# The SSD mixer of an eight-block model: new order of its scalar, vector and matmul work, and the head's own cumulative sum subtracted by matmuls

## The chip, the cores and the metric

The kernel runs on one core of one Trainium2 chip. A core has a matmul engine (PE), a vector engine (DVE), a scalar engine (ACT), a general engine (POOL) and a queue engine that here only issues DMAs (SP). Each runs its own list of instructions in the order in which the program wrote them, and the engines meet only at semaphores. The metric is the device time of one execution in microseconds; smaller is better.

## The reference

The model applies several blocks to an activation of 512 positions by 1024 channels: an SSD mixer with its FFN, an RG-LRU mixer with its FFN, and later blocks of other kinds. Only the SSD mixer is touched. In the names of the kernel it is:

```python
proj = u @ w_in                              # 1024 -> z (2048), xbc (3072), dt (32)
xbc  = silu(causal_dwconv(xbc, conv_w, conv_b))      # 4 taps
xs, bm, cm = split(xbc)                      # 2048 channels, and B and C: 4 groups x 128 each
dt = softplus(dt_raw + dt_bias);  a = -exp(a_log)
cs = cumsum(dt * a) within each chunk of 128 positions    # per head, 32 heads of 64 channels
scores  = (C_l . B_s) * exp(cs_l - cs_s)     # for s <= l in the chunk, else 0
y_diag  = scores @ (xs * dt)
states  = B^T @ (xs * dt * exp(cs_last - cs))
y_off   = exp(cs) * (C @ entering_state)     # states carried over the 4 chunks
y = y_diag + y_off + d_skip * xs
g = y * silu(z);  g = g * rsqrt(mean(g * g) over each group of 512 channels) * norm_w
out = g @ w_out
```

## The kernel before

Activations lie with channels on the 128 partitions and the 512 positions along the free axis. A matmul in float32 is replaced by three in float32r: weight and activation are each split into a high part and a rest, and high x high, high x rest and rest x high are summed. A weight unit is 128 x 1024 (eight blocks of 128 x 128). SP loads it into one of five ring slots when the unit five places earlier is used up, ACT rounds it to the high part (`split_hi`, line 319), POOL subtracts to get the rest (`lows`, line 2335), and PE runs 24 matmuls of 512 columns on it (`pe_tile`, lines 374 to 376).

The mixer has two stretches on PE.

**The convolution stretch.** PE makes 24 tiles of xbc, in turn in PSUM banks 0 to 3. For each tile DVE scales (line 1168, into `ctap`), ACT multiplies by the last tap (line 1024), DVE adds three taps (line 1173) and ACT applies SiLU (line 1015), which frees the bank. The dt work (`dt_chain`: softplus, the cumulative sum `csT`, and its split into three float32r parts in `cs3`) stands as one block on ACT and DVE, ahead of tile 8. After each of the tiles 15 to 22 PE transposes two finished x tiles (`x_natural`, line 839, into banks 4 and 5), and waits before each for the DVE product of the tile two places earlier (line 1152, semaphore `xdt_ok`). DVE does these products behind the convolution of the same turn:

```python
            if 16 <= t:
                x_natural(2 * t - 32)
                x_natural(2 * t - 31)
```

**The pair loop.** Sixteen turns, each for one pair of heads `i` (one tile of 128 channels); four turns make a group. In turn `i` PE does: `y_entering(i)` (line 921), four blocks of z tile `i+1` (`z_blocks`, lines 855 to 857, in PSUM banks 0 and 1 in turn), `y_diagonal(i)` (line 932), `decay_rows(i+1)` (lines 899, 900 and 913) and the other four blocks. `decay_rows` selects the head's row of `cs3` and spreads it over all partitions, adds the causal mask by a second matmul, and for the pair makes the rows for `ec` in bank 6. ACT exponentiates each chunk with the column `nat` (minus the head's own cumulative sum) as its bias: four instructions of 128 columns a head (line 1048). DVE multiplies by C.B (`t1`, line 1235), scales and sums y (1226, 1228, 1210) and gates it with z (`gate`, 1198 to 1203). In turn `i` DVE does the gate of pair `i-1`, behind the products of pair `i`, and that gate frees the bank of z tile `i-1`. Once a group there are `b_natural` (876), `c_b` (867), three `states` (889, between which DVE's `entering` and POOL's `decayed` stand), `squares` (941, 943), `inverse` on ACT and `normed` on DVE. POOL builds `selp` (`pair_rows`), sums squares and makes the rest parts of g (`low_g`).

After the loop `ssd_out` begins (from line 396), and the rest of the program follows.

Of the kernel before, what the change touches and what calls it, by code (L numbers as in the profile page):

```python
# [146 lines left out]
def build_program(nc, dram, out_dram):  # L147
    ctx = ExitStack()
    with ctx:
# [4 lines left out]
        for name, size in (("cols", NCOL * 4 + (-NCOL * 4) % 32), ("ident", 512), ("ones", 512), ("mask_r", 512),  # L154
                           ("neg_diag", 512), ("pair_mask", 512), ("eps", 32), ("x", 16 * KB), ("h", 32 * KB),
                           ("m", 16 * KB), ("raw", 4 * RING * KB), ("whi", 4 * RING * KB), ("nacc", 2 * KB),
                           ("ipre", 2 * KB), ("ident_r", 512), ("sel3", 128), ("sqg", 2 * KB),
# [14 lines left out]
        sel3 = at("sel3", place["sel3"], [P, 32], F32R)  # L172
# [640 lines left out]
        def ssd_pe(pe):  # L813
# [77 lines left out]
            def decay_rows(i):  # L891
# [5 lines left out]
                for e in range(2):  # L897
# [3 lines left out]
                              mask_r[:].unsqueeze(1).broadcast_to((P, NC, P)), start=False, stop=True).then_inc(p_cs, 1)  # L901
# [50 lines left out]
            c_b(0)  # L952
            b_natural(0, 0)
# [35 lines left out]
        def ssd_act(act, own):  # L989
# [3 lines left out]
            def dt_chain():  # L993

                act.wait_ge(dt_dve, 1)
                act.activation(dd[:, 0, :], dd[:, 0, :], ACT.Identity, bias=col("dt_bias")).then_inc(dt_act, 1)
                act.wait_ge(dt_act, 1)
                own.link(act.activation(dd[:, 1, :], dd[:, 0, :], ACT.Abs))
                act.activation(dd[:, 1, :], dd[:, 1, :], ACT.Exp, scale=-1.0).then_inc(dt_act, 1)
                act.activation(acol[:, 0:1], col("a_log"), ACT.Exp).then_inc(dt_act, 1)  # L1000
                act.wait_ge(dt_dve, 2)
                act.activation(dd[:, 3, :], dd[:, 2, :], ACT.Ln).then_inc(dt_act, 1)
                act.wait_ge(dt_dve, 3)
                act.activation(dd[:, 1, :], dd[:, 1, :], ACT.Exp).then_inc(dt_act, 1)

                act.activation(cs3[:], csT[:], ACT.Copy).then_inc(dt_act, 1)
                act.wait_ge(dt_dve, 5)
                act.activation(cs_mid[:], dd[:, 0, :], ACT.Copy).then_inc(dt_act, 1)
                act.activation(cs3[32:64, :], dd[32:64, 0, :], ACT.Copy)
                act.wait_ge(dt_dve, 6)  # L1010
                act.activation(cs3[64:96, :], dd[64:96, 2, :], ACT.Copy).then_inc(dt_act, 1)

            def silu(t):
                act.wait_ge(s_c1, 3 * t + 3)
# [1640 lines left out]
```

## Time and profile before

| | us |
|---|---|
| median of 3 runs | 3316.71 |
| lowest and highest run | 3313.44, 3317.73 |
| the profiled execution's own time | 3312.69 |
| its span, first to last instruction | 3310.8 |
| PE busy in the span | 3030.8 |
| DVE, ACT, POOL busy | 1374.4, 1206.5, 1352.6 |
| convolution stretch, first tiles to its last matmul | until 240.9 |
| pair loop | 257.57 to 518.98 |

A busy share is an average over stages with different limits. PE instructions overlap, so the time of a run of matmuls is read from start to start; the duration of one is longer than its share. The granted clock (PEclk, 1.00 is 2.4 GHz, 0.50 is 1.2 GHz) is a mean over the stretch shown.

### The profile page before, as it was taken

What the parts mean: (1) busy time and instruction counts of PE and PEld (TensorE: products, weight loads), DVE (VectorE), ACT (ScalarE), POOL (GpSimd) and SP (SyncE); (2) the same over time, 40 slices, a digit from 0 to 9 for tenths busy, and PEclk for the clock granted to TensorE, in tenths of its full rate; (3) what the DMA queues carried; (4) which work ended last, traced back from release to release, by engine and by line L of the source; (5) the groups of instructions that cost most, each with busy time, mean ns of one, the idle gap of its engine ahead of it and who ended that gap; (6) DMA issues with size and microseconds to landing.
All of it is one profiled execution on the core that took longest, in us unless ns stands there. A gap on an engine that the chain in (4) does not pass through costs nothing.

```text
span 3310.8 us, 33604 instructions
## 1 busy us (share of the span) xinstructions
PE 3030.8 (92%) x13380; PEld 2459.0 (74%) x13380; DVE 1374.4 (42%) x2011; ACT 1206.5 (36%) x1751; POOL 1352.6 (41%) x724
## 2 busy tenths in 40 slices
PE   8667778999999988899999999798999989999998
PEld 6555557788888766688888877697888866778886
DVE  5533332354154077355145246673422345433132
ACT  5312343543244256354234243103323334343232
POOL 5222225444444436554444444303444443054443
PEclk9878889999999989999999999669999999999999
DMA  3111002222222212222222222001223222022322
GB/s 129 57 38 32 32 26 70 83 96 96 96 96 97 95 58 74 76 96 96 96 96 96 96 83 96 1 1 64 96 88 104 84 85 67 9 92 92 102 91 81
DMA packets 74171, 253.10 MB, mean 76 GB/s; under 512 B 8352, under 2 KB 8352, under 8 KB 74016
## 3 DMA queue, kind: packets, MB, share of 16 engines
q1 hardware_dynamic: 73008, 247.55, 22.8%
q10 hardware_dynamic: 1008, 3.41, 0.3%
q8 instruction: 107, 1.75, 0.2%
q14 instruction: 48, 0.39, 0.0%
HBM read 248.83 MB, written 2.10 MB: 76 GB/s over the span
## 4 chain that ended last, share of the span: by engine, by line
PE 84%; DVE 8%; ACT 3%; issue 2%; DMA 2%; POOL 1%; POOLq 0%; DVEq 0%; ACTq 0%; SPq 0%
PE bank L374 21%; PE bank L375 21%; PE bank L376 21%; PE bank L1639 3%; PE bank L396 2%; PE bank L398 2%; PE bank L397 2%; PE bank L855 1%; PE bank L856 1%; PE bank L857 1%; PE bank L932 1%; POOL wlo L2335 1%; DVE lth L1484 1%; DVE bank L1173 1%; DVE t L1235 1%
## 5 line engine op out<-in xcount | busy, mean ns | idle before, releaser
L2335 POOL TENSOR_TENSOR wlo<-raw,whi 128x1024 fp32r<-128x1024 f32 (+2 forms) x497 | 1133.0, 2282 | 1817.9 <-ACT whi L319 1817.9
L319 ACT ACTIVATE whi<-raw 128x1024 fp32r<-128x1024 f32 (+2 forms) x497 | 500.0, 1007 | 1155.1 <-DMA raw<-in_f_up 490.2
L374 PE MATMUL bank<-h_hi,whi 128*128 128x512 f32 x2240 | 886.9, 396 | 20.8 <-ACT xbc L1015 13.4
L375 PE MATMUL bank<-h_lo,whi 128*128 128x512 f32 x2240 | 879.5, 393 | 0.0
L376 PE MATMUL bank<-h_hi,wlo 128*128 128x512 f32 x2240 | 877.9, 392 | 0.0
L374 PEld LDWEIGHTS bank<-h_hi,whi 128*128 128x128 f32 x2240 | 426.2, 190 | 114.1 <-ACT xbc L1015 14.3
L375 PEld LDWEIGHTS bank<-h_lo,whi 128*128 128x128 f32 x2240 | 426.0, 190 | 90.6 <-issue 2.4
L376 PEld LDWEIGHTS bank<-h_hi,wlo 128*128 128x128 f32 x2240 | 425.5, 190 | 89.9
L374 PE MATMUL bank<-act_hi,whi 128*128 128x512 f32 x864 | 341.3, 395 | 0.8 <-POOL wlo L2335 0.8
L376 PE MATMUL bank<-act_hi,wlo 128*128 128x512 f32 x864 | 341.2, 395 | 0.0
L375 PE MATMUL bank<-act_lo,whi 128*128 128x512 f32 x864 | 341.1, 395 | 0.0
L722 DVE TENSOR_TENSOR tg<-bank,ipre 128x512 f32<-128x512 f32 x108 | 74.6, 691 | 298.3 <-PE bank L376 251.1
L374 PEld LDWEIGHTS bank<-act_hi,whi 128*128 128x128 f32 x864 | 162.3, 188 | 40.3 <-POOL wlo L2335 1.3
L376 PEld LDWEIGHTS bank<-act_hi,wlo 128*128 128x128 f32 x864 | 162.4, 188 | 39.0
L375 PEld LDWEIGHTS bank<-act_lo,whi 128*128 128x128 f32 x864 | 162.4, 188 | 38.8
L855 PE MATMUL bank<-h_hi,whi 128*128 128x512 f32 x128 | 66.5, 520 | 71.3 <-DVE xbc L1203 71.3
L678 ACT ACTIVATE bank<-tg,cols 128x512 f32<-128x512 f32 x108 | 84.6, 783 | 115.9 <-DVE tg L722 115.9
L396 PE MATMUL bank<-h_hi,whi 128*128 128x512 f32 x192 | 82.8, 431 | 42.5 <-DVE h_lo L584 40.8
L742 DVE TENSOR_TENSOR xT<-bank,xT 128x512 f32<-128x512 f32 x32 | 22.1, 692 | 198.8 <-PE bank L376 198.8
L727 DVE TENSOR_TENSOR tv<-bank,ipre 128x512 f32<-128x512 f32 x64 | 44.2, 691 | 133.4 <-PE bank L376 133.4
L855 PEld LDWEIGHTS bank<-h_hi,whi 128*128 128x128 f32 x128 | 30.8, 241 | 85.7 <-DVE xbc L1203 77.9
L708 DVE SCALAR_TENSOR_TENSOR bank<-tg,cols,bank 128x511 f32<-128x511 f32 x108 | 81.5, 755 | 30.6 <-ACT bank L678 29.8
(448 smaller groups left out, 3907.6 us busy)
## 6 DMA issues: line engine op xcount, KB each, us to landing
raw<-in_f_up SPq DMA_DIRECT2D x216, 512.0 KB, 3.5
raw<-in_f_dn SPq DMA_DIRECT2D x64, 512.0 KB, 3.5
raw<-in_ssd_xbc SPq DMA_DIRECT2D x24, 512.0 KB, 3.5
raw<-in_f_dn SPq DMA_DIRECT2D x32, 384.0 KB, 3.0
raw<-in_lru_in SPq DMA_DIRECT2D x20, 512.0 KB, 3.5
raw<-in_ev_in SPq DMA_DIRECT2D x20, 512.0 KB, 3.5
raw<-in_f_dn SPq DMA_DIRECT2D x32, 320.0 KB, 2.9
raw<-in_ssd_z SPq DMA_DIRECT2D x16, 512.0 KB, 3.5
```

What stands on the lines that cost most here:

```text
L319: act.activation(whi[:, s, 0:WIDTH[u]], raw[:, s, 0:WIDTH[u]], ACT.Copy).then_inc(hi_done, 1)
L374: pe.matmul(out, wh, hi, start=kt == 0, stop=False)
L375: pe.matmul(out, wh, lo, start=False, stop=False)
L376: last = pe.matmul(out, wl, hi, start=False, stop=kt == n - 1)
L396: pe.matmul(out, wh, hi, start=kt == 0, stop=False)
L397: pe.matmul(out, wh, lo, start=False, stop=False)
L678: act.activation(bg[:], tg[:, e, :], ACT.Identity, bias=self.prm_col(j + prev, 3), scale=self.prm_col(j + prev, 2)).then_inc(self.tap, 1)
L708: dve.scalar_tensor_tensor(out=dst[:, 1:T], in0=src[:, 0:T - 1], scalar=self.prm_col(j + prev, 4 * v + 1), in1=dst[:, 1:T], op0=ALU.mult, ...
L722: dve.tensor_tensor(tg[:, e, :], bg[:], ipre[:], ALU.mult).then_inc(self.u, 1)
L855: pe.matmul(o, wh, hi, start=kt == 0, stop=False)
L1639: last = pe.matmul(o, wb[rows, n, c, j, :], steps(ev[rows, j, :], m, 1 - n), start=n == 1, stop=n == 0)
L2335: pool.tensor_tensor(wlo[:, s, 0:n], raw[:, s, 0:n], whi[:, s, 0:n].bitcast(F32), ALU.subtract)\
```

## The change

`sel3` gets a second half, columns 32 to 63, with the selection matrix times -1. `decay_rows` adds four float32r matmuls a head, one a chunk: the stationary operand is the chunk of `cs3`, the moving operand the negated selection column spread over 128 columns. They subtract the head's own cumulative sum of each partition. The exponential has no bias any more and is one instruction of 512 columns a head.

The order changes as follows. The dt work is cut into steps ahead of tiles 3, 5, 12, 14, 16 (ACT) and 4, 6 to 11, 13, 15 (DVE). DVE's `x_natural` products stand ahead of the convolution of their turn. B's transposes and C.B of group 0 move between xbc tiles. In the pair loop DVE begins with the two products by C.B, does the whole gate of pair `i` in turn `i` (scale, silu, sum of y, product), and `normed` and `entering` are moved around it. On ACT the exponentials of the heads come ahead of `ec`, and tanh and square are those of pair `i`. On PE `squares` comes a turn earlier; POOL's order follows.

```diff
--- before.py
+++ after.py
...
@@ -898,12 +898,16 @@
                     h = 2 * i + e
                     pe.matmul(bank[4 + e][:], sel3[0:96, h:h + 1].broadcast_to((96, P)), cs3[0:96, :], start=True, stop=False)
                     pe.matmul(bank[4 + e][:].rearrange("p (c l) -> p c l", c=NC), ident_r[:],
-                              mask_r[:].unsqueeze(1).broadcast_to((P, NC, P)), start=False, stop=True).then_inc(p_cs, 1)
+                              mask_r[:].unsqueeze(1).broadcast_to((P, NC, P)), start=False, stop=False)
+                    for c in range(NC):
+                        last = pe.matmul(chunk(bank[4 + e], c), chunk(cs3[0:96, :], c),
+                                         sel3[0:96, 32 + h:33 + h].broadcast_to((96, P)), start=False, stop=c == NC - 1)
+                    last.then_inc(p_cs, 1)
                 g, q = (i - 1) // 4, (i - 1) % 4
                 w(pe, p_ec, i)
                 if i == 0:
                     pe.wait_ge(g_ent, 2)
-                elif q == 1:
+                elif q == 0:
                     w(pe, gn_inv, g)
                 elif q == 2 and g + 1 < SSD_G:
                     pe.wait_ge(g_bn, g + 2)
@@ -949,8 +953,10 @@
                 if 15 <= t <= 22:
                     x_natural(2 * t - 30)
                     x_natural(2 * t - 29)
-            c_b(0)
-            b_natural(0, 0)
+                if t == 20:
+                    b_natural(0, 0)
+                if t == 22:
+                    c_b(0)
             z_blocks(2)
             states(0, 0)
             states(0, 1)
@@ -961,7 +967,7 @@
             for i in range(NX):
                 g, q = i // 4, i % 4
                 y_entering(i)
-                if q == 1 and g:
+                if q == 0 and g:
                     squares(g - 1, i + 1)
                 if q == 2 and g + 1 < SSD_G:
                     b_natural(g + 1, i + 1)
@@ -990,63 +996,65 @@
             stage["ssd_dt"].split_ahead(0)
             st, zt = stage["ssd_xbc"], stage["ssd_z"]
 
...
+            def dt_step(t):
+
+
+                if t == 3:
+                    act.wait_ge(dt_dve, 1)
+                    act.activation(dd[:, 0, :], dd[:, 0, :], ACT.Identity, bias=col("dt_bias")).then_inc(dt_act, 1)
+                    act.wait_ge(dt_act, 1)
+                    own.link(act.activation(dd[:, 1, :], dd[:, 0, :], ACT.Abs))
+                    act.activation(dd[:, 1, :], dd[:, 1, :], ACT.Exp, scale=-1.0).then_inc(dt_act, 1)
+                    act.activation(acol[:, 0:1], col("a_log"), ACT.Exp).then_inc(dt_act, 1)
+                elif t == 5:
+                    act.wait_ge(dt_dve, 2)
+                    act.activation(dd[:, 3, :], dd[:, 2, :], ACT.Ln).then_inc(dt_act, 1)
+                elif t == 12:
+                    act.wait_ge(dt_dve, 3)
+                    act.activation(dd[:, 1, :], dd[:, 1, :], ACT.Exp).then_inc(dt_act, 1)
+                    act.activation(cs3[:], csT[:], ACT.Copy).then_inc(dt_act, 1)
+                elif t == 14:
+                    act.wait_ge(dt_dve, 5)
+                    act.activation(cs_mid[:], dd[:, 0, :], ACT.Copy).then_inc(dt_act, 1)
+                    act.activation(cs3[32:64, :], dd[32:64, 0, :], ACT.Copy)
+                elif t == 16:
+                    act.wait_ge(dt_dve, 6)
+                    act.activation(cs3[64:96, :], dd[64:96, 2, :], ACT.Copy).then_inc(dt_act, 1)
+                    act.wait_ge(tr_dt, 2)
+                    act.activation(etot[:].rearrange("p a b -> p (a b)"), bank[5][:, 0:P], ACT.Exp).then_inc(dt_act, 1)
+
+            def keep_b(g):
+                act.wait_ge(g_bt, g + 1)
+                act.activation(bn[:].rearrange("p c l -> p (c l)"), bank[6][:], ACT.Copy).then_inc(g_bn, 1)
+
+            def keep_cb(g):
+                act.wait_ge(g_cb, g + 1)
+                act.activation(xbc[:, 16 + g, :], bank[7][:], ACT.Copy).then_inc(g_cbm, 1)
 
             def silu(t):
                 act.wait_ge(s_c1, 3 * t + 3)
                 act.activation(xbc[:, t, :], st.bank(t)[:], ACT.Silu).then_inc(st.free(t), 1)
 
             for t in range(24):
-                if t == 8:
-                    dt_chain()
-                if t == 16:
-                    act.wait_ge(tr_dt, 2)
-                    act.activation(etot[:].rearrange("p a b -> p (a b)"), bank[5][:, 0:P], ACT.Exp).then_inc(dt_act, 1)
+                dt_step(t)
                 act.wait_ge(s_u, t + 1)
                 act.activation(st.bank(t)[:], ctap[:, t % 2, :], ACT.Identity, bias=col("ssd_conv", t * 5 + 4),
                                scale=col("ssd_conv", t * 5 + 3)).then_inc(s_tap, 1)
                 st.split_ahead(t)
                 if t:
                     silu(t - 1)
+                if t == 22:
+                    keep_b(0)
             silu(23)
 
...
             def exps(i):
+                for e in range(2):
+                    h = 2 * i + e
+                    act.wait_ge(p_cs, h + 1)
+                    act.activation(bank[4 + e][:], bank[4 + e][:], ACT.Exp).then_inc(p_E, 1)
                 act.wait_ge(p_c2, i + 1)
                 w(act, p_om, i)
                 act.activation(ec[:], bank[6][:], ACT.Exp).then_inc(p_ec, 1)
-                for e in range(2):
-                    h = 2 * i + e
-                    act.wait_ge(p_cs, h + 1)
-                    for c in range(NC):
-                        b = chunk(bank[4 + e], c)
-                        last = act.activation(b, b, ACT.Exp, bias=nat[:, 0, c, h:h + 1])
-                    last.then_inc(p_E, 1)
 
             def z_tanh_of(i):
                 act.wait_ge(z_scaled, i + 1)
@@ -1074,15 +1082,13 @@
                 act.wait_ge(gn_n, j + 1)
                 act.activation(g_hi[:, j, :], xbc[:, j, :], ACT.Copy).then_inc(gn_hi, 1)
 
-            keep_b(0)
             keep_cb(0)
             exps(0)
             for i in range(NX):
                 g, q = i // 4, i % 4
-                if i:
-                    z_tanh_of(i - 1)
-                if q == 1 and g:
+                if q == 0 and g:
                     inverse(g - 1)
+                z_tanh_of(i)
                 if q == 2 and g + 1 < SSD_G:
                     keep_b(g + 1)
                 if q >= 2 and g:
@@ -1092,10 +1098,7 @@
                     exps(i + 1)
                 if q == 2 and g + 1 < SSD_G:
                     keep_cb(g + 1)
-                if i:
-                    square(i - 1)
-            z_tanh_of(NX - 1)
-            square(NX - 1)
+                square(i)
             inverse(SSD_G - 1)
             for k in range(4):
                 high(12 + k)
@@ -1111,38 +1114,49 @@
             st.freed(dve, 0)
             dve.engine_nop().then_inc(dt_dve, 1)
 
...
+            def dt_step(t):
+
...
             st, zt = stage["ssd_xbc"], stage["ssd_z"]
 
@@ -1156,14 +1170,16 @@
 
             for t in range(24):
                 b = st.bank(t)
-                if t == 8:
-                    dt_chain()
+                dt_step(t)
                 if t == 15:
 
                     dve.wait_ge(tr_dt, 1)
                     own.link(dve.tensor_scalar(nat[:, 0].rearrange("p b c -> p (b c)"), bank[4][:, 0:P], -1.0, None, ALU.mult))
                     dve.tensor_copy(nat[:, 1:3].rearrange("p a b c -> p (a b c)"), bank[4][:, P:3 * P]).then_inc(dt_dve, 1)
                     dve.wait_ge(dt_dve, 7)
+                if t >= 16:
+                    x_natural(2 * t - 32)
+                    x_natural(2 * t - 31)
                 st.tile_ready(dve, t)
                 dve.tensor_tensor(ctap[:, t % 2, :], b[:], ipre[:], ALU.mult).then_inc(s_u, 1)
                 dve.wait_ge(s_tap, t + 1)
@@ -1173,13 +1189,10 @@
                     dve.scalar_tensor_tensor(
                         out=b[:, n + 1:T], in0=ctap[:, t % 2, 0:T - n - 1], scalar=col("ssd_conv", t * 5 + 2 - n),
                         in1=b[:, n + 1:T], op0=ALU.mult, op1=ALU.add).then_inc(s_c1, 1)
-                if 16 <= t:
-                    x_natural(2 * t - 32)
-                    x_natural(2 * t - 31)
-
-            def entering(g):
-
-                for z in range(3):
+
+            def entering(g, first, end):
+
+                for z in range(first, end):
                     dve.wait_ge(g_ds, 3 * g + z + 1)
                     if z == 0:
                         dve.tensor_copy(ent[:, 0, :], bank[7][:]).then_inc(g_ent, 1)
...
@@ -1217,31 +1234,35 @@
 
             st.freed(dve, 22)
             dve.memset(bank[2][:, 0:P], 0.0).then_inc(p_xd, 1)
-            entering(0)
+            entering(0, 0, 3)
             y = bank[2][:, P:T]
             for i in range(NX):
                 g, q = i // 4, i % 4
+                dve.wait_ge(g_cbm, g + 1)
+                w(dve, p_y, i)
+                for e in range(2):
+                    dve.wait_ge(p_E, 2 * i + e + 1)
+                    dve.tensor_tensor(t1[:, e, :], bank[4 + e][:], xbc[:, 16 + g, :], ALU.mult).then_inc(p_S, 1)
                 dve.wait_ge(p_off, i + 1)
                 dve.wait_ge(p_ec, i + 1)
                 dve.tensor_tensor(y, y, ec[:, P:T], ALU.mult).then_inc(p_om, 1)
                 dve.wait_ge(p_om, i + 1)
                 dve.scalar_tensor_tensor(out=xbc[:, i, :], in0=xbc[:, i, :], scalar=col("ssd_d", i), in1=bank[2][:],
                                          op0=ALU.mult, op1=ALU.add).then_inc(p_xd, 1)
-                if i:
-                    y_sum(i - 1)
-                dve.wait_ge(g_cbm, g + 1)
-                for e in range(2):
-                    dve.wait_ge(p_E, 2 * i + e + 1)
-                    dve.tensor_tensor(t1[:, e, :], bank[4 + e][:], xbc[:, 16 + g, :], ALU.mult).then_inc(p_S, 1)
-                if i:
-                    gate(i - 1)
-                if q in (1, 2) and g:
-                    normed(4 * g + 2 * q - 6)
-                    normed(4 * g + 2 * q - 5)
+                z_scale(i)
+                if q == 1 and g:
+                    normed(4 * g - 2)
+                    normed(4 * g - 1)
                 if q == 3 and g + 1 < SSD_G:
-                    entering(g + 1)
-            y_sum(NX - 1)
-            gate(NX - 1)
+                    entering(g + 1, 0, 2)
+                z_silu(i)
+                y_sum(i)
+                gated(i)
+                if q == 0 and g:
+                    normed(4 * g - 4)
+                    normed(4 * g - 3)
+                if q == 3 and g + 1 < SSD_G:
+                    entering(g + 1, 2, 3)
             for k in range(4):
                 normed(12 + k)
             so = stage["ssd_out"]
@@ -2398,30 +2419,28 @@
                 if j in (1, 3):
                     u = lows(u, u + 1)
             zt = stage["ssd_z"]
-            u = lows(u, stage["ssd_xbc"].u0 + 23 + RING)
+            u = lows(u, stage["ssd_xbc"].u0 + 20 + RING)
             decayed(0, 0)
             decayed(0, 1)
-            u = lows(u, u + 1)
-            decayed(0, 2)
+            u = lows(u, stage["ssd_xbc"].u0 + 24 + RING)
             pair_rows(0)
             pair_rows(1)
+            decayed(0, 2)
             for i in range(NX):
                 g, q = i // 4, i % 4
-                if i:
-                    u = lows(u, zt.u0 + i + RING)
-                    if i + 1 < NX:
-                        pair_rows(i + 1)
+                if i + 2 < NX:
+                    pair_rows(i + 2)
+                if i and (i - 1) % 4 in (1, 2):
+                    square_sum(i - 1)
+                u = lows(u, zt.u0 + i + 1 + RING)
+                if q == 2 and g + 1 < SSD_G:
+                    decayed(g + 1, 0)
+                    decayed(g + 1, 1)
                 if q >= 2 and g:
                     low_g(4 * g + 2 * q - 8)
                     low_g(4 * g + 2 * q - 7)
-                if q == 2 and g + 1 < SSD_G:
-                    decayed(g + 1, 0)
-                    decayed(g + 1, 1)
                 if q == 3 and g + 1 < SSD_G:
                     decayed(g + 1, 2)
-                if (i - 1) % 4 in (1, 2) and i:
-                    square_sum(i - 1)
-            u = lows(u, zt.u0 + NX + RING)
             for k in range(4):
                 low_g(12 + k)
             u = squares(u, stage["ssd_out"], post0.stat, ffn_pre0.stat)
@@ -2483,7 +2502,8 @@
             act.wait_ge(c_rest, 16)
             act.activation(mask_r[:], pre_mask[:], ACT.Copy)
             act.activation(ident_r[:], ident[:], ACT.Copy)
-            act.activation(sel3[:], pre_sel[:], ACT.Copy)
+            act.activation(sel3[:, 0:32], pre_sel[:], ACT.Copy)
+            act.activation(sel3[:, 32:64], pre_sel[:], ACT.Copy, scale=-1.0)
             norm0.stat.root(act, ipre[:])
             ssd_act(act, own)
             ffn_pre0.act(act, stage["ssd_out"])
```

## Rows read from the trace of the kernel before

**Rows 1.** The page: the chain that ended last, by engine.

```profile
PE 84%; DVE 8%; ACT 3%; issue 2%; DMA 2%; POOL 1%; POOLq 0%; DVEq 0%; ACTq 0%; SPq 0%
```

**Rows 2.** Busy time by stretch: start:end, length, PE, PEld, DVE, ACT, POOL, clock, DMA.

```profile
45.00:86.60 41.60, 40.69 (x180) 33.33 (x178) 25.63 (x33) 23.75 (x30) 17.12 (x8) 1.00 0.28 90
86.60:99.50 12.90, 0.37 (x3) 0.01 (x1) 9.96 (x19) 6.81 (x10) 1.90 (x1) 0.66 0.11 41
130.60:137.46 6.86, 0.04 (x2) 0.04 (x1) 2.95 (x4) 3.88 (x5) 3.78 (x2) 0.83 0.24 76
137.46:240.90 103.44, 70.89 (x256) 57.53 (x257) 29.00 (x42) 17.66 (x22) 18.71 (x10) 0.75 0.11 36
257.57:518.98 261.41, 187.40 (x855) 143.49 (x853) 99.49 (x150) 89.44 (x207) 68.01 (x54) 0.85 0.10 33
```

**Rows 3.** PE's waits (total us, times, longest) in 40:137, 137:257 and 257:519.

```profile
PE bank L374 <- ACT xbc L1015: 13.4, 2, 12.5
...
PE bank L839 <- DVE xdt L1152: 32.5, 7, 4.7
PE bank L839 <- ACT etot L1022: 6.8, 1, 6.8
PE bank L889 <- ACT xbc L1037: 4.1, 1, 4.1
...
PE bank L855 <- DVE xbc L1203: 71.3, 14, 5.9
```

**Rows 4.** Timeline of PE, one transposing turn: start, us, what, count, idle before.

```profile
137.46 1.94 PE L839 MATMUL bank<-ident,xbc 128*128 128x128 f32 x8 [6.82 <-ACT etot L1022]
...
140.05 0.63 PE L376 MATMUL bank<-h_hi,wlo 128*128 128x512 f32 x1
140.47 0.63 PE L374 MATMUL bank<-h_hi,whi 128*128 128x512 f32 x1
...
145.48 0.39 PE L375 MATMUL bank<-h_lo,whi 128*128 128x512 f32 x1
145.71 0.39 PE L376 MATMUL bank<-h_hi,wlo 128*128 128x512 f32 x1
150.75 1.94 PE L839 MATMUL bank<-ident,xbc 128*128 128x128 f32 x8 [4.65 <-DVE xdt L1152]
```

**Rows 5.** Timeline of PE, one turn of the pair loop.

```profile
402.72 1.58 PE L932 MATMUL bank<-t,xdt 128*64 128x128 f32 x16
...
408.24 0.83 PE L921 MATMUL bank<-xbc,ent 128*128 128x128 f32 x6
408.90 1.02 PE L941 MATMUL bank<-nacc,ones 128*128 128x512 f32 x2
409.76 1.02 PE L943 MATMUL bank<-sqg,ones 128*128 128x512 f32 x2
414.98 0.79 PE L855 MATMUL bank<-h_hi,whi 128*128 128x512 f32 x1 [4.20 <-DVE xbc L1203]
```

**Rows 6.** Timeline of PE, between the two stretches.

```profile
241.13 1.06 PE L867 MATMUL bank<-xbc 128*128 128x128 f32 x8
242.02 0.60 PE L876 MATMUL bank<-ident,xbc 128*128 128x128 f32 x4
242.38 0.48 PE L855 MATMUL bank<-h_hi,whi 128*128 128x512 f32 x1
```

**Rows 7.** Groups of instructions in 0:620: busy us, mean ns, idle before.

```profile
L1048 ACT ACTIVATE bank<-bank,nat 128x128 f32<-128x128 f32 x128 | 34.2, 364 | 0.0
...
L2362 POOL TENSOR_TENSOR xdd<-xdt,nat 128x512 f32<-128x512 f32 x12 | 12.3, 1039 | 1.8 <-PE bank L889 1.8
...
L1210 DVE TENSOR_TENSOR xbc<-bank,xbc 128x512 f32<-128x512 f32 x16 | 10.9, 684 | 0.0
...
L1042 ACT ACTIVATE ec<-bank 128x512 f32<-128x512 f32 x16 | 9.6, 598 | 112.9 <-PE bank L913 112.9
```

**Rows 8.** Busy time of a stretch of the last attention block, columns as in rows 2.

```profile
2799.00:2879.00 80.00, 77.06 (x409) 56.28 (x407) 47.73 (x161) 33.78 (x101) 0.74 (x1) 1.00 0.00 1
```

More of the change, by code:

```diff
@@ L171, in build_program @@
         ident_r = at("ident_r", place["ident_r"], [P, P], F32R)
[L172 removed]
+        sel3 = at("sel3", place["sel3"], [P, 64], F32R)
         sqg = at("sqg", place["sqg"], [P, T])
@@ L991, in ssd_act @@
             st, zt = stage["ssd_xbc"], stage["ssd_z"]
[L993 to L1011, printed above, removed]
@@ new lines, in dt_step @@
+            def dt_step(t):
+                if t == 4:
+                    dve.wait_ge(dt_act, 2)
+                    dve.tensor_scalar(v, u, 1.0, None, ALU.add).then_inc(dt_dve, 1)
+                elif t == 6:
+                    dve.wait_ge(dt_act, 4)
+                    own.link(dve.tensor_scalar(v, v, -1.0, 1e-30, ALU.add, ALU.max))
+                    own(dve.reciprocal(v, v))
+                elif t == 7:
+                    own.sync()
+                    own.link(dve.tensor_tensor(ln, ln, u, ALU.mult))
+                    own(dve.tensor_tensor(ln, ln, v, ALU.mult))
+                elif t == 8:
+                    own.sync()
+                    own.link(dve.tensor_scalar(v, u, -0.5, 1.0, ALU.mult, ALU.add))
+                    own(dve.tensor_tensor(v, v, u, ALU.mult))
+                elif t == 9:
+                    own.sync()
+                    own.link(dve.tensor_tensor(ln, ln, v, ALU.max))
+                    own(dve.scalar_tensor_tensor(out=dtT[:], in0=x, scalar=0.0, in1=ln, op0=ALU.max, op1=ALU.add))
+                elif t == 10:
+                    dve.wait_ge(dt_act, 3)
+                    own.link(dve.tensor_scalar(acol[:, 1:2], acol[:, 0:1], -1.0, None, ALU.mult))
+                    own.link(dve.tensor_scalar(x, dtT[:], acol[:, 1:2], None, ALU.mult))
+                    for c in range(NC):
+                        own(dve.tensor_tensor_scan(out=chunk(csT[:], c), data0=ones[:], data1=chunk(x, c), initial=0.0,
+                                                   op0=ALU.mult, op1=ALU.add))
+                elif t == 11:
+                    own.sync()
+                    cs3d = csT[:].rearrange("p (c l) -> p c l", c=NC)
+                    tot = cs3d[:, :, P - 1:P]
+                    dve.tensor_tensor(dd[:, 1, :].rearrange("p (c l) -> p c l", c=NC), tot.broadcast_to((P, NC, P)), cs3d,
+                                      ALU.subtract).then_inc(dt_dve, 1)
+                    dve.tensor_tensor(diag[:], ident[0:32, 0:32].unsqueeze(2).broadcast_to((32, 32, NC)),
+                                      tot[0:32].rearrange("p c l -> p l c").broadcast_to((32, 32, NC)),
+                                      ALU.mult).then_inc(dt_dve, 1)
+                elif t == 13:
+                    dve.wait_ge(dt_act, 6)
+                    dve.tensor_tensor(x, csT[:], cs3[:].bitcast(F32), ALU.subtract).then_inc(dt_dve, 1)
+                elif t == 15:
+                    dve.wait_ge(dt_act, 7)
+                    dve.tensor_tensor(v, x, cs_mid[:].bitcast(F32), ALU.subtract).then_inc(dt_dve, 1)
```

45 lines of the change are left out of this document (6 added, 39 removed).

## The prediction

> **What bounds the kernel now.** I read the page's chain first: PE ends most of it [rows 1]. Then the busy time by stretch, for where PE is not dense: in 45 to 86.6 us it is busy throughout at clock 1.00, but from 86.6 to 99.5 it stands, from 137.46 to 240.9 it is busy 71 of 103 us at clock 0.75, and in the pair loop 187 of 261 us at 0.85, with no other engine over 100 us [rows 2]. So neither stretch is bounded by an engine's work; both are bounded by waits. PE's waits give their names: 13.4 us for xbc's SiLU (the dt block on ACT and DVE), 6.8 us for `etot`, 32.5 us in 7 waits for the product `xdt`, 71.3 us in 14 waits for the gate of line 1203 [rows 3]. Last the timelines of PE. A wait costs more than its idle time: after one, the matmuls start 0.43 us apart (1.2 GHz), and only later 0.23 us apart (2.4 GHz) [rows 4]. Behind the mixer PE is dense, so what the mixer saves moves the end.
>
> **The dt steps.** The block's 12.9 us stall [rows 2] and the slow start behind it (about 8 matmuls 0.2 us too long, 1.6 us) go. The cover: before the block DVE was busy 25.6 us of 41.6 and ACT 23.8 us [rows 2]. A tile lasts 24 x 0.227 = 5.45 us, so DVE has about 2.1 us to spare in each. The block's DVE work, some 15 us (10.0 of it in the stall's row [rows 2]), is spread over 12 tiles with 25 us to spare, and a tile's bank is needed again only four tiles later. ACT switches its function table more often, inside the same slack. If that cover failed, up to 14.5 us would stay. The steps end with `etot` behind the tap and the weight split of tile 15, as before, and one more full-width copy stands ahead of it (0.6 us, as `ec` of [rows 7]): the wait of 6.9 us becomes 7.5. Sum: -12.9 - 1.6 + 0.6 = **-13.9 us** (ends: 0 and -20.8, the latter if the second wait went too).
>
> **The products `xdt` ahead of the convolution.** PE asks, before the transposes behind tile t, for products that DVE now does before it starts tile t's convolution, while PE makes that tile. The 4.65 us wait [rows 4] goes, and the clock stays up. One turn was 150.75 - 137.46 = 13.3 us [rows 4]. Eight transposes take about 8 x 0.11 = 0.9 (four take 0.36 in [rows 6]); with the tile, 6.35 us. DVE's turn is two products and five passes with a wait for ACT, about 5.3 us by 0.68 a pass [rows 7], so DVE does not become late. The first turn still starts slow: 13.3 - 4.65 = 8.65. With C.B and the transposes of B, now inside this stretch (0.89 and 0.36 [rows 6]): 8.65 + 7 x 6.35 + 1.25 = 54.3 against 103.4 [rows 2], **-49.1 us**. At 8.65 for all eight it would be -33. Between the stretches PE still waits for tile 23's SiLU and C.B's copy; it merely arrives earlier. I take 16.7 + 0.4 us there, **+0.4**.
>
> **The added matmuls.** Eight a pair, 128 in all, 96 x 128 by 128 columns in float32r. No row shows that shape. Below: the stream of 128 columns at the 512-column pitch of [rows 4] would be 0.227 / 4 = 0.06 us. Above: the whole 0.227. I take 0.111, the pitch of the 128-column instructions of line 867 (eight in 0.89 us [rows 6]), the nearest in shape: 0.89 us a pair, 14.2 us in all (7 to 29). The Trainium skill, "TensorE: Matmul & The Clock Gate", section "Back-to-back issue gap", gives about 81 ns for a 128-column matmul in a stream of load and matmul pairs; by that it would be 10.4 us. Its figure is not for float32r, and the row stands.
>
> **The pair loop.** Before, z tile i+1 waited for the gate of pair i-1, which DVE did in the same turn behind y_entering, the sum and the products. Now that gate ends in turn i-1. I walk a turn from the end of `y_diagonal(i-1)`, T. DVE: sum and gate, T+1.8; products of pair i need the exponentials. PE: selection, mask and new matmuls, the first head at about T+1.0, the second T+1.9, `ec`'s row T+2.1. ACT: each exponential 0.6 us at full width [rows 7] in place of four of 128 columns, so T+1.8 and T+2.7. DVE's products end at T+3.6. PE meanwhile has four z blocks, y_entering and four more, and wants the products at T+8.3. The gate that z tile i+1 needs was done at T+1.8, and is wanted at T+5.4. Queued behind DVE's new wait on the exponentials are y's scaling, the skip and the z scale; they would be late only if the exponentials came over 2 us later. So PE should be its own bound. Its turn without waits, at full clock: y_diagonal, decay_rows and four blocks 408.24 - 402.72 = 5.52, y_entering 0.66 [rows 5], four blocks 2.72, new matmuls 0.89: 9.8 us. DVE's work is 99.5 / 16 = 6.2 us a turn, ACT's 5.6, POOL's 4.3 [rows 2], all below.
>
> Fifteen turns 147; the last, without z blocks, 2.1; three times a group's own work (squares 1.72 and three states at 0.86 [rows 5], C.B and B 1.25 [rows 6], 5.55) 16.7. What is late next is POOL: `decayed(g+1, 2)` (1.04 us [rows 7]) stands behind the weight rest and two `low_g`, and PE wants its state right behind decay_rows; I allow 2 us in two groups, 4. Sum 170 against 261.4, **-91.6 us**. Here the shorter exponentials and `ec` being last cost nothing, hidden by PE's z blocks; without that cover the turn would be longer by their 1.8 us. The loads of SP follow the end of each tile and land before ACT's tanh, as before. The tail into `ssd_out` is bounded by PE's own first twelve blocks, so it is unchanged; the added table copy at the start lies in ACT's wait for PE.
>
> **Sum.** -13.9 - 49.1 + 0.4 - 91.6 = -154.2. Against the profiled execution (3312.7) that is 3158.5; the median of the runs is 4.0 above it (3316.7), so the forecast is **3163 us**.
>
> **Rivals.** (a) *Narrow matmuls cost as much as wide ones*, 0.227 us each: +14.9, **3178**. For: float32r is a mode of its own, and no narrow one is in the trace. Against: other 128-column instructions take half.
> (b) *A wait stays in the loop.* A turn has many crossings between four queues, and a late tanh (behind the weight split's DMA on ACT) or the products hold the gate. If half of the 5.1 us wait stays in 15 turns, 38 us, with some slow restart, 10: **3211**. For: DVE and ACT are strict queues and the walk leaves out latencies. Against: 3 us and more of room at each crossing.
> (c) *The clock stays at 1.2 GHz among transposes.* Seven turns would have 24 matmuls 0.2 us longer and transposes 0.9 longer, 5.7 x 7 = 40: **3203**. In this stretch the clock was 0.75 [rows 2], but the rows put the slow matmuls behind the waits; in the last attention, where transposes stand among matmuls without long waits, it is 1.00 [rows 8]. The same page of the Trainium skill, "Part 4: PE-mode transpose", says that transposing does not count as busy for the clock; by that rule this case would hold, and the last row speaks against it.
> (d) *The dt steps stall the tiles*: the ACT queue with its table switches falls behind by more than the four banks, and the 14.5 us stay: **3178**.
> (e) *Slower than before*: each new matmul holds PE, in that its stationary operand can't be brought in beside the open sum of the bank. It decides from 154 / 128 = 1.2 us each; at 1.3 us instead of 0.111 the time is 3163 + 152 = 3315, at 1.4 **3328**. The longest PE instruction in these rows takes 1.02 for two, so nothing speaks for it. That the change leaves the waits as they are (no order that PE sees altered) can be excluded only by the code: it would give about 3317 + 14 = 3331, with (e)'s side.
>
> **Chances.** Forecast 0.60 (its own range 3148 to 3175), (a) 0.14, (b) 0.13, (c) 0.05, (d) 0.05, (e) and no effect 0.03. The low end takes 0.06 us a matmul (-7), no POOL wait (-4) and the `etot` wait gone (-7): 3145, and I go to 3140; the high end takes in (a), (c), (d) and (b): 3213. Two runs of this kernel can be told apart from about 0.2%, 6.6 us: faster 0.97, within 0.2% 0.01, slower 0.02.
>
> **What would show it.** In the new profile: no wait over 2 us of line 374 before tile 16; one wait of some 7.5 us before the first transposes, none for `xdt`; turns of 6.4 us; clock 1.00 from there; turns of the pair loop of 9.8 us with no wait of the z blocks; the narrow matmuls 0.11 us apart; a wait of states for `xdd` in two or three groups. The forecast is wrong if the loop still shows z waits for the gate, or PE waits for the products by C.B, or the clock falls in it.

## The result and the profile after

The changed kernel takes **3148.2 us** (median; 3143.5 to 3150.8) against 3315.8 beside it: ratio **0.949** [0.948, 0.951]. The forecast of 3163 lies 14.8 us above it. The profiled execution took 3148.6 us, with a span of 3146.7 (before 3310.8). The page of the kernel after, the chain by engine, answers to [rows 1]:

```profile
PE 86%; DVE 7%; ACT 3%; DMA 1%; issue 1%; POOL 1%; POOLq 0%; DVEq 0%; ACTq 0%; SPq 0%
```

The busy time by stretch, columns as in [rows 2]. The first stretch is that of before's stall; then come the wait for `etot`, the turns with transposes, and the pair loop:

```profile
86.60:99.50 12.90, 12.09 (x53) 9.48 (x52) 10.95 (x17) 4.49 (x6) 5.00 (x3) 1.00 0.29 87
121.20:128.07 6.87, 0.00 (x1) 0.03 (x1) 2.49 (x4) 4.51 (x6) 3.34 (x2) 0.78 0.26 76
128.07:181.96 53.89, 53.89 (x268) 45.63 (x269) 30.39 (x44) 18.18 (x23) 18.71 (x9) 0.96 0.21 69
199.60:374.31 174.71, 171.45 (x975) 137.65 (x973) 98.63 (x151) 76.78 (x118) 70.56 (x55) 0.98 0.15 47
```

103.4 us became 53.9 and 261.4 became 174.7, with PE busy nearly throughout. PE's waits of the whole span, those in the mixer, answer to [rows 3]:

```profile
PE bank L839 <- ACT etot L1024: 7.4, 1, 7.4
...
PE bank L889 <- POOL xdd L2383: 3.3, 2, 1.7
...
PE bank L824 <- ACT dd L1014: 1.9, 1, 1.9
...
PE bank L374 <- ACT xbc L1036: 1.7, 2, 0.9
```

The 32.5 us for `xdt` and the 71.3 us for the gate are gone. PE's timeline of the first and second transposing turn (start, us, what, count), against [rows 4]:

```profile
128.07 1.94 PE L839 MATMUL bank<-ident,xbc 128*128 128x128 f32 x8 [7.44 <-ACT etot L1024]
...
131.09 0.63 PE L374 MATMUL bank<-h_hi,whi 128*128 128x512 f32 x1
...
136.27 1.03 PE L839 MATMUL bank<-ident,xbc 128*128 128x128 f32 x8
...
142.62 0.60 PE L839 MATMUL bank<-ident,xbc 128*128 128x128 f32 x4
```

After the one wait the granted clock is 0.50 (1.2 GHz) for 3.5 us. Then a turn takes 142.62 - 136.27 = 6.35 us, as forecast. PE's timeline of a turn of the pair loop, against [rows 5], with line 903 the new matmuls:

```profile
199.60 0.83 PE L925 MATMUL bank<-xbc,ent 128*128 128x128 f32 x6
200.18 0.48 PE L855 MATMUL bank<-h_hi,whi 128*128 128x512 f32 x1
...
203.13 1.58 PE L936 MATMUL bank<-t,xdt 128*64 128x128 f32 x16
204.64 0.50 PE L899 MATMUL bank<-cs,sel 96*128 96x512 f32 x1
204.98 0.40 PE L900 MATMUL bank<-mask_r,ident_r 128*128 128x512 f32 x1
205.21 0.56 PE L903 MATMUL bank<-sel,cs 96*128 96x128 f32 x4
205.60 0.45 PE L899 MATMUL bank<-cs,sel 96*128 96x512 f32 x1
205.89 0.40 PE L900 MATMUL bank<-mask_r,ident_r 128*128 128x512 f32 x1
...
209.53 0.72 PE L925 MATMUL bank<-xbc,ent 128*128 128x128 f32 x5
```

The blocks of z follow without a wait, and a turn takes 209.53 - 199.60 = 9.93 us. From the first of four narrow matmuls to the wide one behind them are 0.39 us, and the next wide one starts 0.29 us later in place of 0.23: 0.45 us for four, 0.11 us each.

Where the 164.1 us of span went, stage by stage, each from the starts of its first PE instructions:

| stage | before | after | change | forecast |
|---|---|---|---|---|
| to the first transposes | 137.5 | 128.1 | -9.4 | -13.9 |
| transposing turns | 103.4 | 53.9 | -49.5 | -49.1 |
| between | 16.7 | 17.6 | +1.0 | +0.4 |
| pair loop, to `ssd_out` | 261.4 | 174.7 | -86.7 | -91.6 |
| all behind | 2791.8 | 2772.4 | **-19.4** | 0 |

The last row is the surprise: 19.4 us in code that the change doesn't touch. Two groups of the page, before and after, show one place of it (busy us, mean ns of one):

```profile
L374 PE MATMUL bank<-act_hi,whi 128*128 128x512 f32 x864 | 341.3, 395 | 0.8 <-POOL wlo L2335 0.8
```

```profile
L374 PE MATMUL bank<-act_hi,whi 128*128 128x512 f32 x864 | 336.2, 389 | 0.9 <-POOL wlo L2356 0.9
```

The same 864 matmuls take 6 ns less each, though clock and shape are the same. Lines 375 and 376 show the same. What did change for them is the place of `act_hi`: `sel3` grew from 128 to 256 bytes a partition, and what comes behind it moved by 128, the large buffer that holds `act_hi` and `act_lo` among it.

### The profile page after: what moved, and what is told of

Same layout as the page of the kernel before. It is cut to its first block, busy times and chain, and to the rows that moved or that the text cites. A ratio compares the mean times of both kernels' runs of the same rounds, so it can differ in the third digit from the quotient of the medians.

```text
span 3146.7 us, 33766 instructions
## 1 busy us (share of the span) xinstructions
PE 2977.8 (95%) x13508; PEld 2440.9 (78%) x13508; DVE 1379.6 (44%) x2011; ACT 1194.0 (38%) x1658; POOL 1352.2 (43%) x724
## 4 chain that ended last, share of the span: by engine, by line
PE 86%; DVE 7%; ACT 3%; DMA 1%; issue 1%; POOL 1%; POOLq 0%; DVEq 0%; ACTq 0%; SPq 0%
PE bank L374 22%; PE bank L375 22%; PE bank L376 22%; PE bank L1660 3%; PE bank L396 2%; PE bank L397 2%; PE bank L398 2%; PE bank L855 1%; PE bank L857 1%; PE bank L856 1%; POOL wlo L2356 1%; PE bank L936 1%; DVE bank L1189 1%; DVE lth L1505 1%; ACT whi L319 1%
## 5 line engine op out<-in xcount | busy, mean ns | idle before, releaser
L374 PE MATMUL bank<-h_hi,whi 128*128 128x512 f32 x2240 | 880.2, 393 | 9.2 <-DVE h_lo L1956 3.4
L374 PEld LDWEIGHTS bank<-h_hi,whi 128*128 128x128 f32 x2240 | 422.3, 189 | 102.1 <-DVE h_lo L1956 4.2
L396 PE MATMUL bank<-h_hi,whi 128*128 128x512 f32 x192 | 80.6, 420 | 42.7 <-DVE h_lo L584 41.0
L529 POOL TENSOR_TENSOR nacc<-nacc,sqb 128x512 f32<-128x512 f32 x65 | 86.2, 1326 | 16.8 <-ACT sqb L511 15.9
L1660 PE MATMUL bank<-ev,wb 32*128 32x64 f32 x512 | 88.8, 373 | 3.1 <-DVE wb L1874 3.1
```

Of the source, the lines that this page charges most:

```text
L374: pe.matmul(out, wh, hi, start=kt == 0, stop=False)
L396: pe.matmul(out, wh, hi, start=kt == 0, stop=False)
L529: pool.tensor_tensor(nacc[:], nacc[:], sqb[:, (j + 1) % 2, :], ALU.add).then_inc(s_acc, 1)
L1660: last = pe.matmul(o, wb[rows, n, c, j, :], steps(ev[rows, j, :], m, 1 - n), start=n == 1, stop=n == 0)
```

## The experiments

Ratios are to the kernel before on the same chip. The first question was the 19 us.

**Padding only.** The kernel before, with 128 unused bytes behind `sel3`:

```diff
-("sel3", 128)
+("sel3", 256)
```

> The kernel before with 128 bytes of padding behind sel3, nothing else. The changed kernel gained 144.6 us up to the end of the pair loop and 19.5 us more behind it, in code that was not edited. Theory P (place): the growth of sel3 from 128 to 256 bytes moved everything behind it by 128 bytes, the activations act_hi and act_lo among them, and matmuls that stream those start 0.227 us apart in place of 0.233. Then this kernel gains about 19 us, some 3297 against 3316, with the mixer as it was, and L374 on act_hi falls from 395 to about 389 ns. Rival C (carry-over): the later stages run faster because the mixer ends earlier or denser (clock, order of DMAs). Then this kernel takes 3316, as before.

Measured: 3292.3 us, **0.9945** [0.993, 0.996], mixer end at 517.1 (before 519.0). The change's place in memory alone is worth 22 us by the medians (3314.2 beside it) and 18 by the ratio, in a kernel that has nothing else of it. The 1.9 us at the mixer's end are no part of that for sure: with all buffers moved, below, it ends at 517.4 and gains nothing.

**The change at the old distance.** The kernel after, with another 128 bytes:

```diff
-("sel3", 256)
+("sel3", 384)
```

> The changed kernel with another 128 bytes behind sel3, so that the large buffer stands at 192 modulo 256 again, as before the change. Theory P: it loses the gain behind the loop, about 3148 + 19 = 3167, and the mixer takes what it takes in the changed kernel. Rival C: 3148. A second rival, P2 (only the exact old place is slow, not the residue): 3148 too, with e1 at 3297.

Measured: 3163.1 us, 0.9555 [0.954, 0.957]: 14.9 us come back. By the two profiled executions it is 17.2 behind the mixer, while the mixer ends 3.1 us sooner (371.2 for 374.3), as the clock didn't fall behind its second wait for `xdd` (see the run with `decayed` first). PE's timelines, first of the padded kernel before, then of this one, show the pitch, 0.227 against 0.233 us at full clock:

```profile
1119.94 0.39 PE L374 MATMUL bank<-act_hi,whi 128*128 128x512 f32 x1
1120.17 0.39 PE L375 MATMUL bank<-act_lo,whi 128*128 128x512 f32 x1
```

```profile
1000.14 0.39 PE L374 MATMUL bank<-act_hi,whi 128*128 128x512 f32 x1
1000.37 0.40 PE L375 MATMUL bank<-act_lo,whi 128*128 128x512 f32 x1
```

**Everything moved.** The kernel before with all buffers 128 bytes further, so that distances stay:

```diff
-base = 16512
+base = 16640
```

> The kernel before with every buffer of SBUF 128 bytes higher, so that all distances between buffers are as before, and the large buffer alone changes nothing against the weights' ring. If the place counts absolutely (theory P, form a), the large buffer is now at 64 modulo 256 and its matmuls are fast, while h_hi and h_lo, now at 192, become slow: 2240 x 3 matmuls by 0.006 us, 40 us slower, less 19 gained: about 3337. If it counts relative to the weights that are loaded at the same time (form b), nothing changes: 3316. Rival C: 3316 too, which e1 tells apart.

Measured: 3313.7 us, 1.0001 [0.999, 1.001], 395 ns for `act_hi`. It is the distance from other buffers, not the address itself. The likeliest partner is the weights' buffers, which stayed while the moving operands moved: `h_hi` and `h_lo`, a multiple of 256 bytes from them in every version, kept the pitch of 0.227 us in all of them. The runs don't single the weights out from the other buffers ahead of `sel3`, so this is not shown.

**Half the padding.** 64 bytes in place of 128:

```diff
-("sel3", 128)
+("sel3", 192)
```

> The kernel before with 64 bytes of padding, so that the large buffer stands 64 bytes modulo 256 below the weights' ring, where before it stood at 128 and in e1 at 0. Theory b1 (only a distance of 128 modulo 256 is slow): as e1, 3292. Theory b2 (any distance but 0 is slow): as before, about 3315. b3 (the further, the slower): between the two.

Measured: 3312.4 us, 0.9992 [0.998, 1.000], 394 ns. The gain doesn't come in part: of the distances tried, counted from the weights' buffers modulo 256, 0 is fast, 128 and 192 are slow.

**The order alone.** The kernel after without the new matmuls, with before's exponentials and their bias (the second half of `sel3` stays, and with it the place):

```diff
-mask_r[:]..., start=False, stop=False)
-for c in range(NC): last = pe.matmul(chunk(bank[4 + e], c), ...)
-last.then_inc(p_cs, 1)
+mask_r[:]..., start=False, stop=True).then_inc(p_cs, 1)
...
-act.activation(bank[4 + e][:], bank[4 + e][:], ACT.Exp)
+for c in range(NC): act.activation(b, b, ACT.Exp, bias=nat[:, 0, c, h:h + 1])
```

> The changed kernel (its place of the buffers too) with the bias exponentials back and the negated matmuls left out: the reorder alone. Theory B (the loop is PE's own): a turn loses the 0.98 us that the eight narrow matmuls take in its trace, 16 in the loop; ACT's two heads take 2.1 in place of 1.2 us, which has 3 us and more of room before PE wants the products. So about 3148 - 16 = 3132, with turns of 8.95 us. Rival R: the shorter exponentials are what keeps PE dense; without them DVE's products come late, PE waits in each turn, and the time is 3148 or more.

Measured: 3132.4 us, **0.9454** [0.944, 0.947]: 16 us faster than the whole change. PE's timeline of this kernel, a turn of the loop:

```profile
347.86 0.83 PE L921 MATMUL bank<-xbc,ent 128*128 128x128 f32 x6
...
352.90 0.50 PE L899 MATMUL bank<-cs,sel 96*128 96x512 f32 x1
353.24 0.39 PE L900 MATMUL bank<-mask_r,ident_r 128*128 128x512 f32 x1
...
356.90 0.83 PE L921 MATMUL bank<-xbc,ent 128*128 128x128 f32 x6
```

Turns are 356.90 - 347.86 = 9.04 us. The exponentials of 128 columns make ACT busy 91.3 us in this loop (198.4 to 359.2) in place of 76.8, and that costs nothing: PE waits for none of them. The new matmuls take 9.93 - 9.04 = 0.89 us a turn, 14 us in 16 pairs.

**The matmuls alone**, in before's order, with the padding:

> The kernel before, padded as in e1 (3292), with the negated matmuls and full-width exponentials but in the old order. Theory B: the narrow matmuls stand on PE between y_diagonal and y_entering, which the old loop's chain runs through, so all of their 15.7 us show: about 3308. Rival R: the old loop has 71 us of waits in which they vanish, and ACT's exponentials get shorter: 3292 or less.

Measured: 3309.6 us, 0.9985 [0.997, 1.000]; against the padded kernel before (3292.3) that is 17 us slower by the medians, 13 by the ratios. Its waits of PE show that the gate still holds the loop as in [rows 3]:

```profile
PE bank L855 <- DVE xbc L1204: 71.3, 14, 5.9
```

Its loop takes 275.9 us where the padded kernel's takes 258.9. So its 14 us of matmuls are added in full; where the other 3 come from is not shown. ACT is busy 74.0 us in the loop in place of 89.8, and that did not help.

**The matmuls three times** (subtract, add, subtract, which computes the same):

```diff
-for c in range(NC): ... sel3[0:96, 32 + h:33 + h]
+for r, sign in enumerate((32, 0, 32)):
+    for c in range(NC): ... sel3[0:96, sign + h:sign + h + 1]
```

> The changed kernel with the narrow matmuls three times (subtract, add, subtract), 256 more of them. In its trace four of them took 0.39 us from the first's start to the next matmul's. By that PE's own time grows by 256 x 0.098 = 25 us, and as the loop is PE's own, all of it shows: 3173. Rival: the other engines have room enough that part of it vanishes, or a pass of 12 on one open sum costs more than its share: at 0.227 each it would be 3206.

Measured: 3171.0 us, 0.9577 [0.956, 0.959], +22.8 us, mixer end +20.7. PE's timeline:

```profile
205.31 1.45 PE L904 MATMUL bank<-sel,cs 96*128 96x128 f32 x12
206.60 0.45 PE L899 MATMUL bank<-cs,sel 96*128 96x512 f32 x1
```

Twelve take 206.60 - 205.31 = 1.29 us where four take 0.39: 0.1125 us for one more, 28.8 us for all 256. About 8 of these don't show: PE now comes late enough that its waits for `xdd`, with their slow clock, vanish (6.9 us, see the run with `decayed` first), and the first transposes came 1.0 us sooner in this execution.

**Products behind the convolution again**, the rest of the change kept:

```diff
+                if t >= 16:
+                    x_natural(2 * t - 32)
+                    x_natural(2 * t - 31)
```

(behind the taps, and taken out ahead of `tile_ready`)

> The changed kernel with DVE's xdt products behind the convolution of their turn again. By the forecast's second term the seven waits of 4.65 us and the slow clock behind them come back, turns of 13.4 us in place of 6.34: 7 x 7.1 = 50 us, about 3198. Rival: with the rest of the order changed DVE is early enough and only part comes back, under 3175.

Measured: 3201.3 us, 0.9662 [0.965, 0.968], mixer end +50.6. Its transposes, as a group in 0:620:

```profile
L839 PE MATMUL bank<-ident,xbc 128*128 128x128 f32 x64 | 15.5, 424 | 40.0 <-DVE xdt L1166 32.5 <-ACT etot L1024 7.4
```

The same 32.5 us as before. The other 18 us go with the clock: 0.76 over 128.84 to 240 us here. This one move is worth all that its stage gained.

**The dt steps in one block** ahead of tile 8, the rest kept:

```diff
-dt_step(t)
+if t == 8:
+    for k in (...): dt_step(k)
```

> The changed kernel with the dt steps of tiles 3 to 15 in one block ahead of tile 8 again, the last ACT step left ahead of tile 16. The first transposes came 9.4 us earlier in the changed kernel (128.07 against 137.46), where the forecast had 13.9. Theory: that is what the spreading is worth, and the time is about 3148 + 9.5 = 3158. Rival: spreading is worth the forecast's 13.9 and something else in the changed kernel costs 4.5 us before tile 16, so 3162; or the block is covered now, 3148.

Measured: 3156.2 us, 0.9525 [0.951, 0.954]: 8.0 us more. PE's stall of 12.4 us is back, and the first transposes start at 137.9, 9.9 us later than in the kernel after. So spreading the steps is worth 8 to 10 us, not 14. This kernel also shows a part of why. DVE's timelines: the steps in the block, while POOL is idle, then the same first ones in the kernel after:

```profile
84.94 0.69 DVE L1132 TENSOR_TENSOR dd<-dd 128x512 f32<-128x512 f32 x1
...
86.40 0.43 DVE L1136 TENSOR_SCALAR dd<-dd 128x512 f32<-128x512 f32 x1
```

```profile
62.52 0.69 DVE L1184 TENSOR_TENSOR ctap<-bank,ipre 128x512 f32<-128x512 f32 x1
...
72.85 2.33 DVE L1189 SCALAR_TENSOR_TENSOR bank<-ctap,cols,bank 128x511 f32<-128x511 f32 x3 [0.85 <-ACT bank L1041]
75.09 1.73 DVE L1128 TENSOR_TENSOR dd<-dd 128x512 f32<-128x512 f32 x1
...
77.46 0.68 DVE L1184 TENSOR_TENSOR ctap<-bank,ipre 128x512 f32<-128x512 f32 x1
...
81.24 1.46 DVE L1132 TENSOR_SCALAR dd<-dd 128x512 f32<-128x512 f32 x1
...
83.34 0.68 DVE L1184 TENSOR_TENSOR ctap<-bank,ipre 128x512 f32<-128x512 f32 x1
```

and POOL's of the kernel after:

```profile
61.31 2.40 POOL L2356 TENSOR_TENSOR wlo<-raw,whi 128x1024 fp32r<-128x1024 f32 x1 [2.76 <-ACT whi L319]
...
73.88 2.39 POOL L2356 TENSOR_TENSOR wlo<-raw,whi 128x1024 fp32r<-128x1024 f32 x1 [6.09 <-ACT whi L319]
...
80.02 2.40 POOL L2356 TENSOR_TENSOR wlo<-raw,whi 128x1024 fp32r<-128x1024 f32 x1 [3.75 <-ACT whi L319]
```

The first instruction of a step takes 1.03 us longer than in the block (1.73 against 0.69, 1.46 against 0.43), and it ends shortly after POOL's subtraction does (76.82 against 76.27; 82.70 against 82.42). It is so, within 0.03 us, in the steps ahead of tiles 4, 6 to 9, 11 and 13; in that ahead of tile 10 it is 0.80 us, on its second instruction, and the step ahead of tile 15, which starts 0.46 us before POOL's subtraction, keeps its 0.68. The passes that read a bank keep their time beside a subtraction: line 1184 at 62.52, line 1189 at 72.85. The Trainium skill, "SBUF — State Buffer", section "SBUF: two separate sides", says that VectorE and GpSimd share a pair of ports, which the one that starts first holds for its whole instruction, against a VectorE instruction with two SBUF inputs or in a two-port mode. The rows agree within 0.15 us: 76.27 + 0.69 = 76.96 and 82.42 + 0.43 = 82.85. Line 1128 has two SBUF inputs; line 1132 has one, and no row shows in which mode it runs.

**`decayed(g+1, 2)` ahead of the two `low_g`** on POOL:

```diff
+                if q == 3 and g + 1 < SSD_G:
+                    decayed(g + 1, 2)
                 if q >= 2 and g:
                     low_g(4 * g + 2 * q - 8)
                     low_g(4 * g + 2 * q - 7)
-                if q == 3 and g + 1 < SSD_G:
-                    decayed(g + 1, 2)
```

> The changed kernel with POOL's decayed(g+1, 2) ahead of its two low_g instead of behind them. In the changed kernel PE waits twice for it (1.57 and 1.70 us), and the second wait is followed by 7 us at 1.2 GHz; those two groups are 1.9 and 4.9 us longer than the first. Theory: both waits and the slow stretch go, 3148 - 6.7 = 3141. Rival: low_g then comes late, and ssd_out or the high parts wait for it; 3148.

Measured: 3141.2 us, 0.9472 [0.946, 0.949], mixer end -6.9. Both waits for `xdd` went. They were 3.3 us of idle time; the rest was the clock behind the second. PE's timelines, of the kernel after and then of the version at the old distance:

```profile
286.60 1.13 PE L889 MATMUL bank<-xdd,bn 128*128 128x512 f32 x2 [1.57 <-POOL xdd L2383]
...
333.90 2.07 PE L889 MATMUL bank<-xdd,bn 128*128 128x512 f32 x2 [1.70 <-POOL xdd L2383]
...
336.20 0.63 PE L856 MATMUL bank<-h_lo,whi 128*128 128x512 f32 x1
```

```profile
333.77 1.13 PE L889 MATMUL bank<-xdd,bn 128*128 128x512 f32 x2 [1.64 <-POOL xdd L2383]
...
334.96 0.39 PE L856 MATMUL bank<-h_lo,whi 128*128 128x512 f32 x1
```

The two computed the same up to there, and the clock fell in one and not in the other: 334.96 - 333.77 = 1.19 us to line 856 against 2.30. It fell in the run with the products behind (1.62 us idle), not in that with the dt block (1.68) or the order alone (2.70).

**The best version**: the order alone, `decayed` first, and `etot` at ACT's step 14, with the last copy into `cs3` at 15:

```diff
                 elif t == 14:
...
+                    act.wait_ge(tr_dt, 2)
+                    act.activation(etot[:]..., bank[5][:, 0:P], ACT.Exp).then_inc(dt_act, 1)
-                elif t == 16:
+                elif t == 15:
```

> The reorder alone (3132), with decayed first as in e8, the exponential etot ahead of tile 14 and the last copy of cs3 ahead of tile 15. PE's waits there were 5.2 us in two for xdd and 7.5 us for etot. Theory: decayed first gives 5 to 8, etot early gives 6 and up to 2 us of slow clock: about 3119. Rival: PE only meets the next thing, the copy of cs3 or the tanh's queue, and stays above 3126.

Measured: **3123.5 us**, 0.9419 [0.940, 0.944], 24.7 us below the change as it stands. The first transposes start 4.6 us earlier, and behind the shorter wait the clock stays up (1.06 us for eight, 1.94 in the kernel after):

```profile
123.44 1.06 PE L839 MATMUL bank<-ident,xbc 128*128 128x128 f32 x8 [2.83 <-DVE nat L1177]
```

## Why the prediction came out as it did

The time lay in the range and the mechanism of the mixer was right, but the total hides two misses of opposite sign. The stages of the mixer gave 144.7 us where 154.2 were forecast, and 19.4 came from a place that the forecast had at nothing: 154.2 - 9.5 + 19.4 = 164.1. That the second more than paid for the first is luck. So is it that the version at the old distance takes 3163.1, the forecast to the microsecond: in it the mixer gained 147.8 us and what lies behind it 2.2, 4.2 less than forecast in all, and the forecast had added 4.0 us for the median over the profiled execution, which are 0.5 there.

- **The dt steps, -13.9 forecast, -9.4 measured.** The step that failed is the cover: "DVE has about 2.1 us to spare in each". The spare time was too large, since it was taken from DVE's busy time: in each tile DVE also stands 0.85 us for ACT's tap (the row at 72.85), so a tile takes it 3.77 us (from line 1184's start at 44.36 to that at 48.13) and leaves 1.7. And the durations of the steps were read where they ran alone. Among the tiles most are held 1.03 us, and a turn of DVE takes 83.34 - 77.46 = 5.9 us, over PE's 5.45. DVE's lag reaches PE through ACT, in the kernel after:

```profile
102.47 0.78 ACT L1041 ACTIVATE bank<-ctap,cols 128x512 f32<-128x512 f32 x1 [3.46 <-DVE ctap L1184]
...
106.03 0.63 ACT L1014 ACTIVATE dd<-dd 128x512 f32<-128x512 f32 x1
```

```profile
106.72 0.43 PE L824 MATMUL bank<-ident,csT 32*128 32x32 f32 x4 [1.92 <-ACT dd L1014]
...
108.42 0.63 PE L375 MATMUL bank<-h_lo,whi 128*128 128x512 f32 x1
108.84 0.63 PE L376 MATMUL bank<-h_hi,wlo 128*128 128x512 f32 x1
```

  PE waited 1.9 us here and 0.8 at 99.1 (the 1.7 of the waits above holds 0.9 that stood at 48.6 in the kernel before too), and behind the 1.9 eight matmuls are 0.43 us apart: the slow start of 1.6 us, which the forecast had as gone, only moved. These make the 4.5 us. That the lags come wholly from POOL's subtractions was not tried. The `etot` wait came as forecast (7.4 for 7.5).
- **The products ahead, -49.1 forecast, -49.5 measured.** Turn 6.35 for 6.35, and undoing it alone gave back 50.6.
- **The narrow matmuls, 0.111 us each.** Measured 0.111 in place and 0.1125 by tripling them. The nearest row in shape was the right one to choose. The about 81 ns of the Trainium skill, "TensorE: Matmul & The Clock Gate", section "Back-to-back issue gap", would have been 4 us too low.
- **The pair loop, -91.6 forecast, -86.7 measured.** No z block waits for the gate and the group's own work is 5.55 us as worked out. A turn is 9.93, not 9.8 (2.0 us in 15: the four z blocks behind y_entering take 203.13 - 200.18 = 2.95 us, not 2.72), and POOL's waits cost 6.7, not 4: 3.3 idle, the rest the slow clock, which the forecast left out and which came in some executions only. They stood where the forecast had put them, and taking them away gave 6.9.
- **All behind, 0 forecast, -19.4 measured.** "What the mixer saves moves the end" held; that nothing else moves did not. The diff showed `sel3` growing, and the prediction took a buffer's place to be without a price.

Of the rivals: (a) falls with 0.111 us. (b) falls, as no wait of the loop names the gate; what stays there is 3.3 us for `xdd`. (c) falls: PE's granted clock over the transposing turns behind the first is

```profile
136.27:181.96 45.69, 45.69 (x237) 38.72 (x236) 29.00 (x42) 18.18 (x23) 18.71 (x9) 1.00 0.25 81
```

and the rule of the Trainium skill, "TensorE: Matmul & The Clock Gate", section "Part 4: PE-mode transpose", that transposing does not count as busy for the clock, shows no effect in this mixture of 8 transposes to 24 matmuls. (d) came in part: 4.5 of the 14.5 us, with the lag starting on DVE. (e) falls: 0.111 is far below 1.2.

Open is why the distance between two buffers changes the pitch of a matmul; the placements tried say only that it does. The matmuls in place of the biases are a loss of 16 us, because ACT had room and PE had none: of the edits, the reorder alone brings the gain, beside what the new place gives.

## What to carry to other kernels

Work that moves from an engine with room to the engine that ends everything costs its full time: price the move alone, apart from the reorder that it comes with. An idle gap on PE can cost the slow matmuls behind it as well as its length, so an order that has the operand ready a few microseconds sooner can be worth more than the wait it names. Room on an engine is its time from one tile to the next, not what its busy share leaves. And before crediting a change with its gain, pad the old kernel to the new layout: here 20 of 168 us were the buffer's place.

## What was not expected of the hardware

- 512-column matmuls with the moving operand 128 bytes (or 192, modulo 256) off the distance at which they are fast are 0.233 us apart in place of 0.227; over the kernel 15 to 22 us of 3300.
- A DVE instruction that reads and writes SBUF alone was held up 1.03 us beside POOL's subtraction of 128 x 1024 when that had started first, in seven of nine steps (0.80 in one, nothing in the one that started ahead of it); those that read a bank weren't.
- A narrow float32r matmul of 96 rows by 128 columns costs 0.1125 us in a group of four (0.39 us, and 0.06 more at the next wide one) and in a group of twelve (1.29 and 0.06).
- The same short wait in the same place cost the clock in two executions (1.70 us idle, then 6 us at 1.2 GHz, some 3 us lost; 1.62 idle, 3.4 us, 1.6 lost) and not in three others (1.64, 1.68, 2.70).
